# Stick-breaking attention: the two heads of a pair taken alternately, block by block, in the score and the value products

## The chip, the cores and the metric

The kernel runs on one core of a Trainium2 chip. The metric is the device time of one execution in microseconds (us), the median of several runs. PE is TensorE (matmuls), ACT is ScalarE, DVE is VectorE, POOL is GpSimd, SP is SyncE, which only issues transfers here.

## The reference, cut to what matters

The model is a stack of three blocks over 512 positions of width 1024. The first block's mixer has four retention heads and eight stick-breaking heads of width 64; the change touches only the latter.

```python
def stick_breaking(q, k, v):                      # (B, S, H, D) with S = 512, H = 8, D = 64
    ...
        z = jnp.einsum('bhid,bhsd->bhis', qi, kh).astype(jnp.float32) * scale
        past = (kpos[None, :] < qpos[:, None])[None, None]
        log_keep = jnp.where(past, jax.nn.log_sigmoid(-z), 0.0)
        between = lax.cumsum(log_keep, axis=3, reverse=True) - log_keep
        a = jnp.where(past, jnp.exp(jax.nn.log_sigmoid(z) + between), 0.0)
        return jnp.einsum('bhis,bhsd->bhid', a.astype(vh.dtype), vh)
```

## The kernel before

Everything is written by hand: each stage gives one function per engine, the functions of a block run one after another on their engine, and semaphores tie them together. No scheduler moves anything.

`stick_stage` takes the eight heads as four pairs `p`. A pair's queries `q` and keys `kk` lie on 128 partitions, head 0 of the pair on 0 to 63 and head 1 on 64 to 127; `v` has positions on the partitions, head 0 in columns 0 to 63 and head 1 in 64 to 127. On PE a pair goes through:

- scores (line 480): for each head `hh` and key block `j` (128 keys), one product of 64 partitions into 512, 384, 256 or 128 causal columns, into three PSUM banks of its own (0 to 2 for head 0, 3 to 5 for head 1). Before that PE waits for `y_out`, since the result of the pair before lies in banks 0 and 3, and head by head.
- the projections of the next pair (`project`, lines 448 and 454; parts 0, 1, 2 are q, k, v) into banks 6 and 7. Part 2 waits until ACT has moved part 0 out of its bank (`kept`).
- sums (line 493): the cumulative sums over the keys, ten products per head, after `cut`.
- values (line 503): for each head, four products of 128 partitions and 64 columns of `v` into PSUM partitions 0 to 63 of bank 0 (head 0) or 64 to 127 of bank 3 (head 1). They wait for `masked`, head by head.

Beside this ACT computes, for each head, Abs, Exp and Ln of its scores (lines 534, 536, 538), DVE adds the positive part (line 582), POOL zeroes what isn't in the past (line 558, `cut`); after the sums ACT takes the Exp (line 546) and POOL masks it (line 565, `masked`). DVE copies each head's values out of PSUM (line 574, `y_out`). ACT moves q, k (line 516) and v (line 523) out of PSUM. In fp32 the program's one matmul appears in the trace as two passes, each with its own weight load, so that the eight score products of a pair are 16 rows there.

After the last pair comes `mix_out_stage` (line 614), whose products wait for all eight `y_out`. The odd block later in the program has a product of the same kind as the scores: `score` (line 1139) issues the products of two 64-partition halves right behind each other into two banks.

Of the kernel before, what the change touches and what calls it, by code (L numbers as in the profile page):

```python
# [15 lines left out]
P = 128  # L16
S = 512
NT = S // P
# [124 lines left out]
def slab_ready(k, pe, slab, turn=0):  # L143
    slot, _, before, dmas, per = slab
    pe.wait_ge(k.landed[slot], turn * (16 * dmas * per) + 16 * (before + dmas))
# [252 lines left out]
def stick_stage(k):  # L398
# [12 lines left out]
    scored, logged, softened, cut = k.sem("sb_scored"), k.sem("sb_logged"), k.sem("sb_softened"), k.sem("sb_cut")  # L411
    summed, exped, masked = k.sem("sb_summed"), k.sem("sb_exped"), k.sem("sb_masked")
    valued, y_out = k.sem("sb_valued"), k.sem("sb_y_out")
    k.sb_y_out = y_out
    place = [(0, 0), (1, 0), (2, 0), (1, 384)]
# [9 lines left out]
    def tensor(pe):  # L425
        def project(p, part):
            n = 3 * p + part
            slabs = k.sb_slabs[p]
            if n >= 2:

                if part == 2:
                    pe.wait_ge(kept, 2 * p + 1)
                elif part == 0:
                    pe.wait_ge(kept, 2 * p)
                else:
                    pe.wait_ge(v_kept, p)
            elif part == 0:
                pe.wait_ge(k.ret_kept, 16)
                pe.wait_ge(k.ret_rotated, 16)
            bank = 6 + (n % 2)  # L440
            for c in range(KC):
                slab = slabs[c // 4]
                if part == 0 and c % 4 == 0:
                    slab_ready(k, pe, slab)
                w = k.ring[:, slab[0], 0:4 * 3 * P].rearrange("p (k n) -> p k n", k=4)[:, c % 4, :]
                w = w[:, part * P:(part + 1) * P]
                if part < 2:
                    mm = pe.matmul(PS[:, bank, :], w, k.XT[:, c, :], start=(c == 0), stop=(c == KC - 1))
            if part == 2:
                for t in range(NT):  # L450
                    for c in range(KC):
                        slab = slabs[c // 4]
                        w = k.ring[:, slab[0], 0:4 * 3 * P].rearrange("p (k n) -> p k n", k=4)[:, c % 4, :]
                        mm = pe.matmul(PS[:, bank, t * P:(t + 1) * P], k.XT[:, c, t * P:(t + 1) * P],
                                       w[:, 2 * P:3 * P], start=(c == 0), stop=(c == KC - 1))
                        if t == NT - 1 and c == 3:
                            mm.then_inc(k.freed[slabs[0][0]], 1)
            mm.then_inc(projected, 1)
            if part == 2:
                pe.drain().then_inc(k.freed[slabs[1][0]], 1)  # L460

        pe.wait_ge(k.cols_in, 1)
        pe.wait_ge(k.taps_in, 1)
        for part in range(3):
            project(0, part)
        pe.wait_ge(k.bias_masked, 1)
        for p in range(4):
            pe.wait_ge(kept, 2 * p + 2)
            for hh in range(2):
                if p > 0:  # L470
                    pe.wait_ge(y_out, 2 * (p - 1) + hh + 1)
                elif hh == 0:
                    pe.wait_ge(k.ret_masked, 16)
                    pe.wait_ge(k.ret_normed, 4)
                    pe.wait_ge(k.ret_y_out, 4)
                r = slice(64 * hh, 64 * hh + 64)
                for j in range(NT):
                    bank, col = place[j]
                    n = S - j * P
                    mm = pe.matmul(PS[:, 3 * hh + bank, col:col + n], kk[r, j * P:(j + 1) * P],  # L480
                                   q[r, j * P:S], start=(j != 3), stop=False, skip_group_check=True)
                mm.then_inc(scored, 1)
            if p < 3:
                for part in range(3):
                    project(p + 1, part)
            for hh in range(2):
                pe.wait_ge(cut, 2 * p + hh + 1)
                for j in range(NT):
                    bank, col = place[j]
                    for j2 in range(j, NT):  # L490
                        lo = (j2 - j) * P
                        n = S - j2 * P
                        mm = pe.matmul(PS[:, 3 * hh + bank, col + lo:col + lo + n],
                                       k.negtri if j2 == j else k.negone,
                                       soft[hh][:, COL[j2]:COL[j2] + n],
                                       start=False, stop=(j2 == NT - 1), skip_group_check=True)
                mm.then_inc(summed, 1)
            pe.wait_ge(v_kept, p + 1)
            for hh in range(2):
                pe.wait_ge(masked, 2 * p + hh + 1)  # L500
                r = slice(64 * hh, 64 * hh + 64)
                for j in range(NT):
                    mm = pe.matmul(PS[r, 3 * hh, j * P:S], v[:, j, r],
                                   a[hh][:, COL[j]:COL[j] + S - j * P],
                                   start=(j == 0), stop=(j == NT - 1), skip_group_check=True)
                mm.then_inc(valued, 1)

    def scalar(act):
        def keep(p):
# [59 lines left out]
    def vector(dve):  # L569
# [6 lines left out]
        for p in range(4):  # L576
# [6 lines left out]
            keep_y(p)  # L583

    return dict(sync=sync, tensor=tensor, scalar=scalar, vector=vector, gpsimd=gpsimd)

def mix_out_stage(k, name, w_out, slabs, ready, gains, mode, beside=None):
# [1987 lines left out]
```

## Time and profile before

| | |
|---|---|
| time, median of 3 runs | 2657.3 us (2656.2, 2657.3, 2662.22) |
| span of the profiled execution | 2660.7 us |
| profiled execution's own time | not listed apart; it can't be shorter than its span, so of the three only 2662.22 could be it |
| PE busy | 2367.5 us (89%) |
| DVE, ACT, POOL busy | 925.8, 685.3, 258.9 us |
| stretch of the stick-breaking scores to values | 196.42 to 341.62 us of the span |

How to read it: the page lists for each engine how long it was busy, and the timeline of one engine lists its groups of instructions in order with the idle time before each and what ended it. Neighbouring rows give the cost of a stage on PE best, as the difference of their starts: matmuls are pipelined and the tail of one lies under the next. PEclk is the clock that PE was granted, 1.00 for 2.4 GHz and 0.50 for 1.2 GHz.

### The profile page before, as it was taken

Reading aid. Unit: us, or ns where it says so; the run is one execution under the profiler, and the core shown is the slowest. Engines: PE = TensorE matmul, PEld = TensorE weight load, DVE = VectorE, ACT = ScalarE, POOL = GpSimd, SP = SyncE. Lnnn points to the kernel's source line nnn. Section 1 sums busy time; section 2 is a strip of 40 time slices with the busy share of each in tenths; the row PEclk is TensorE's granted clock in tenths of the full one; section 3 lists DMA queues with packets and bytes.
Section 4 is the critical chain, followed back from the end, with each engine's and each line's share of the span. In section 5 each row is a group of like instructions: output and inputs, shape, how many; then the busy total and the mean of one; then the engine's idle time right before and its main releaser. Section 6 shows DMA issues by size and latency. Waiting matters only on the chain. (4 is left out here: it accounts for less than half of the span.)

```text
span 2660.7 us, 25189 instructions
## 1 busy us (share of the span) xinstructions
PE 2367.5 (89%) x9090; PEld 1526.2 (57%) x9090; DVE 925.8 (35%) x1587; ACT 685.3 (26%) x930; POOL 258.9 (10%) x303
## 2 busy tenths in 40 slices
PE   8989899999979888999999784868489999999994
PEld 4456548888865555478888573654344444444442
DVE  1221135465333333355653559873300001000002
ACT  1114404344212333043432232323011111111111
POOL 1000100000000000000000035760100000000001
PEclk9999999999989999899999897879699999999997
DMA  9021108432225002043322141101099898979893
GB/s 264 24 88 39 41 16 323 136 95 97 89 72 155 32 33 64 0 119 95 96 95 95 48 111 36 48 16 35 17 386 339 307 344 290 346 290 344 300 334 139
DMA packets 286099, 385.91 MB, mean 145 GB/s; under 512 B 13512, under 2 KB 181628, under 8 KB 285880
## 3 DMA queue, kind: packets, MB, share of 16 engines
q1 hardware_dynamic: 268872, 323.54, 36.9%
q0 software_dynamic: 17136, 61.14, 6.2%
q8 instruction: 59, 0.97, 0.2%
q14 instruction: 32, 0.26, 0.0%
HBM read 347.89 MB, written 39.37 MB: 146 GB/s over the span
## 5 line engine op out<-in xcount | busy, mean ns | idle before, releaser
L845 PE MATMUL PS<-XS,split 128*128 128x512 f32 (+1 forms) x2304 | 486.1, 374 | 13.0 <-DVE split L157 9.9
L845 PEld LDWEIGHTS PS<-XS,split 128*128 128x128 f32 x2304 | 410.2, 191 | 88.6 <-issue 10.3
L2241 PE MATMUL PS<-ring,W 128*128 128x512 f32 x960 | 424.5, 598 | 6.9 <-ACT W L2287 6.9
L2241 PEld LDWEIGHTS PS<-ring,W 128*128 128x128 f32 x960 | 179.6, 191 | 223.3 <-issue 209.3
L157 DVE TENSOR_TENSOR split<-ring,split 128x2048 fp32r<-128x2048 f32 x68 | 155.7, 2292 | 219.9 <-ACT split L152 219.9
L2262 PE MATMUL PS<-ring,W 128*128 128x512 f32 x480 | 212.4, 595 | 11.3 <-ACT W L2297 11.3
L878 PE MATMUL PS<-split,XS 128*128 128x512 f32 x960 | 218.4, 389 | 0.3 <-DVE XS L157 0.3
L878 PEld LDWEIGHTS PS<-split,XS 128*128 128x128 f32 x960 | 180.0, 188 | 38.4 <-issue 1.1
L152 ACT CAST split<-ring 128x2048 fp32r<-128x2048 f32 x78 | 148.1, 1903 | 154.4 <-PE PS L878 110.8
L2314 DVE TENSOR_TENSOR W<-PS,W 128x512 f32<-128x512 f32 x30 | 20.8, 692 | 450.6 <-PE PS L2241 450.6
L614 PE MATMUL PS<-ring,W 128*128 128x512 f32 x384 | 170.3, 603 | 2.9 <-issue 0.8
L2262 PEld LDWEIGHTS PS<-ring,W 128*128 128x128 f32 x480 | 90.0, 190 | 122.4 <-issue 122.4
L1440 PE MATMUL PS<-XS,split 128*128 128x512 f32 x432 | 105.5, 405 | 24.6 <-DVE W L1753 17.3
L614 PEld LDWEIGHTS PS<-ring,W 128*128 128x128 f32 x384 | 73.5, 194 | 93.3 <-issue 90.2
L1119 PE MATMUL PS<-XT,ring 128*128 128x512 f32 x256 | 121.6, 631 | 2.0 <-PEq L2558 2.0
L263 PE MATMUL PS<-ring,XT 128*128 128x512 f32 x256 | 111.4, 593 | 1.0 <-DMA ring<-in_w_in_even 0.8
L1440 PEld LDWEIGHTS PS<-XS,split 128*128 128x128 f32 x432 | 84.2, 197 | 44.8 <-issue 20.0
L2320 DVE COPY W<-PS 128x512 f32<-128x512 f32 x60 | 38.7, 686 | 198.0 <-PE PS L2262 198.0
L1507 DVE SCALAR_TENSOR_TENSOR W<-W,chan 128x512 f32<-128x512 f32 x90 | 105.0, 1167 | 7.2 <-issue 0.4
L921 ACT ACTIVATE W<-PS,taps 128x512 f32<-128x512 f32 x88 | 67.4, 777 | 142.8 <-PE PS L845 142.7
L1119 PEld LDWEIGHTS PS<-XT,ring 128*128 128x128 f32 x256 | 51.0, 205 | 70.9 <-issue 70.5
L948 DVE SCALAR_TENSOR_TENSOR W<-PS,taps,W 128x511 f32<-128x511 f32 x88 | 65.6, 746 | 70.9 <-ACT W L921 70.9
(337 smaller groups left out, 2341.3 us busy)
## 6 DMA issues: line engine op xcount, KB each, us to landing
ring<-in_expert_w_gate SPq DMA_DIRECT2D x60, 1024.0 KB, 14.5
ring<-in_expert_w_up SPq DMA_DIRECT2D x60, 1024.0 KB, 15.4
ring<-in_expert_w_down SPq DMA_DIRECT2D x60, 1024.0 KB, 14.8
ring<-in_w_up SPq DMA_DIRECT2D x88, 512.0 KB, 5.1
ring<-in_w_down SPq DMA_DIRECT2D x44, 512.0 KB, 4.3
expert_rows<-rows POOLq DMA_DIRECT2D x4, 4096.0 KB, 30.4
expert_rows<-W POOLq DMA_DIRECT2D x30, 512.0 KB, 7.1
ring<-in_w_in_even SPq DMA_DIRECT2D x56, 256.0 KB, 5.3
```

Source lines behind the costliest of these rows:

```text
L152: act.copy(hi, raw).then_inc(sem, 1)
L157: return dve.tensor_tensor(lo, raw, hi.bitcast(F32), ALU.subtract)
L263: mm = pe.matmul(PS[:, 4 + t, :], k.XT[:, c, t * P:(t + 1) * P], w, start=(c == 0), stop=(c == KC - 1))
L614: mm = pe.matmul(k.PS[:, 2 * (t % 2) + half, :], YT[:, c, t * P:(t + 1) * P], w[:, 512 * half:512 * half + 512], start=(c == 0), stop=(c = ...
L845: mm = pe.matmul(PS[:, b + q, rows], w[:, c, q, :], x_half(k, high)[:, c, rows], start=(c == 0 and m == 0), stop=(c == KC - 1 and m == 2))
L878: mm = pe.matmul(PS[:, 2 * t + half, :], h_half(i, high)[:, at:at + P], w[:, c, 512 * half:512 * half + 512], start=(i == 0 and c == 0 and ...
L921: act.activation(conv[:, i % 2, q, :], PS[:, b + q, :], ACT.Identity, bias=tap_at(k, layer, 3, q, turn, i), scale=tap_at(k, layer, 2, q, t ...
L1119: mm = pe.matmul(PS[:, bank, :], view[c // 4][:, c % 4, part, :], k.XT[:, c, :], start=(c == 0), stop=(c == KC - 1))
L1440: mm = pe.matmul(to, part[:, c, columns], x_half(k, high)[:, c, rows], start=(c == 0 and m == 0), stop=(c == KC - 1 and m == 2))
L1507: mm = eng.scalar_tensor_tensor(acc[:, c, :], u[:, c, i - 1:i - 1 + S], wide[:, i - 1, c:c + 1], acc[:, c, :], ALU.mult, ALU.add)
L2241: mm = pe.matmul(PS[:, 2 * b + m, :], xT[b][:, 4 * half + c, :], w[:, c, :], start=(half == 0 and c == 0), stop=(half == 1 and c == 3))
L2262: mm = pe.matmul(PS[:, bank, :], midT[b][:, 2 * half + c, :], w[:, c, 512 * side:512 * side + 512], start=(half == 0 and c == 0), stop=(ha ...
```

## The change

In the scores and in the values the loop over the blocks is now outside and the loop over the two heads inside. So each head's product for a block stands right behind the other head's for the same block. The waits, which were one for each head, become one for the pair ahead of the first product: scores wait until both `y_out` of the pair before are there, values until both heads are masked. The increments (`scored`, `valued`) stay at each head's last product, which are now next to each other. ACT, DVE and POOL are unchanged.

```diff
-            for hh in range(2):
-                if p > 0:
-                    pe.wait_ge(y_out, 2 * (p - 1) + hh + 1)
-                elif hh == 0:
-                    pe.wait_ge(k.ret_masked, 16)
...
-                r = slice(64 * hh, 64 * hh + 64)
-                for j in range(NT):
-                    bank, col = place[j]
-                    n = S - j * P
+            if p > 0:
+                pe.wait_ge(y_out, 2 * p)
...
+            for j in range(NT):
+                bank, col = place[j]
+                n = S - j * P
+                for hh in range(2):
+                    r = slice(64 * hh, 64 * hh + 64)
                     mm = pe.matmul(PS[:, 3 * hh + bank, col:col + n], kk[r, j * P:(j + 1) * P],
                                    q[r, j * P:S], start=(j != 3), stop=False, skip_group_check=True)
-                mm.then_inc(scored, 1)
+                    if j == NT - 1:
+                        mm.then_inc(scored, 1)
...
             pe.wait_ge(v_kept, p + 1)
-            for hh in range(2):
-                pe.wait_ge(masked, 2 * p + hh + 1)
-                r = slice(64 * hh, 64 * hh + 64)
-                for j in range(NT):
+            pe.wait_ge(masked, 2 * p + 2)
+            for j in range(NT):
+                for hh in range(2):
+                    r = slice(64 * hh, 64 * hh + 64)
                     mm = pe.matmul(PS[r, 3 * hh, j * P:S], v[:, j, r],
                                    a[hh][:, COL[j]:COL[j] + S - j * P],
                                    start=(j == 0), stop=(j == NT - 1), skip_group_check=True)
-                mm.then_inc(valued, 1)
+                    if j == NT - 1:
+                        mm.then_inc(valued, 1)
```

On PE, from the values of pair 0 to the first projection of pair 2, the order before is (the shapes are those of the output; in brackets the semaphores waited for):

```order
135 L503 MATMUL PS<-W 64x512 [waits sb_masked,sb_v_kept]
136 L503 MATMUL PS<-W 64x384
137 L503 MATMUL PS<-W 64x256
138 L503 MATMUL PS<-W 64x128
139 L503 MATMUL PS<-W 64x512 [waits sb_masked]
...
142 L503 MATMUL PS<-W 64x128
143 L480 MATMUL PS<-W 128x512 [waits sb_y_out,sb_kept]
...
146 L480 MATMUL PS<-W 128x128
147 L480 MATMUL PS<-W 128x512 [waits sb_y_out]
...
151 L448 MATMUL PS<-XT,ring 128x512 [waits slab_landed0,sb_kept]
```

At the same place the order after is:

```order
132 L504 MATMUL PS<-W 64x512 [waits sb_masked,sb_v_kept]
133 L504 MATMUL PS<-W 64x512
134 L504 MATMUL PS<-W 64x384 x2
135 L504 MATMUL PS<-W 64x256 x2
136 L504 MATMUL PS<-W 64x128 x2
137 L480 MATMUL PS<-W 128x512 [waits sb_y_out,sb_kept]
138 L480 MATMUL PS<-W 128x512
139 L480 MATMUL PS<-W 128x384 x2
140 L480 MATMUL PS<-W 128x256 x2
141 L480 MATMUL PS<-W 128x128 x2
142 L448 MATMUL PS<-XT,ring 128x512 [waits slab_landed0,sb_kept]
```

The second wait for `sb_masked` has moved ahead of all eight value products, the second wait for `sb_y_out` ahead of all eight score products, and the heads alternate. Nothing else has moved on any engine.

## Rows read from the trace of the kernel before

**Rows 1.** The page: busy time of each engine over the span, and its share.

```profile
PE 2367.5 (89%) x9090; PEld 1526.2 (57%) x9090; DVE 925.8 (35%) x1587; ACT 685.3 (26%) x930; POOL 258.9 (10%) x303
```

**Rows 2.** Timeline of PE, the stick-breaking stage: start, us, group, [idle before, releaser].

```profile
196.42 4.00 PE L480 MATMUL PS<-W 64*128 64x512 f32 x16 [0.36 <-issue]
200.36 14.00 PE L448 MATMUL PS<-XT,ring 128*128 128x512 f32 x32
214.19 7.31 PE L454 MATMUL PS<-ring,XT 128*128 128x128 f32 x64
...
230.47 4.86 PE L503 MATMUL PS<-W 128*64 128x512 f32 x16
235.26 4.03 PE L480 MATMUL PS<-W 64*128 64x512 f32 x16
239.22 14.00 PE L448 MATMUL PS<-XT,ring 128*128 128x512 f32 x32
253.06 7.31 PE L454 MATMUL PS<-ring,XT 128*128 128x128 f32 x64
...
323.31 6.73 PE L493 MATMUL PS<-W,small 128*128 128x512 f32 x20 [6.29 <-POOL W L558]
331.40 4.60 PE L493 MATMUL PS<-W,small 128*128 128x512 f32 x20 [1.36 <-POOL W L558]
335.93 4.86 PE L503 MATMUL PS<-W 128*64 128x512 f32 x16
341.62 18.69 PE L614 MATMUL PS<-ring,W 128*128 128x512 f32 x43 [0.83 <-issue]
```

**Rows 3.** Timeline of PE's weight loads, second head's values of pair 0.

```profile
232.96 0.19 PEld L503 LDWEIGHTS PS<-W 128*64 128x64 f32 x2 [0.37 <-POOL W L565]
```

**Rows 4.** Timeline of ACT in the stage.

```profile
230.58 1.24 ACT L546 ACTIVATE W<-PS 128x1280 f32<-128x1280 f32 x1 [3.10 <-PE PS L493]
...
237.72 1.24 ACT L534 ACTIVATE W<-PS 128x1280 f32<-128x1280 f32 x1 [1.71 <-PE PS L480]
...
250.90 0.58 ACT L516 ACTIVATE W<-PS 128x512 f32<-128x512 f32 x1
```

**Rows 5.** Timeline of POOL, second head's mask of pair 0.

```profile
231.88 1.03 POOL L565 TENSOR_SCALAR_AFFINE_SELECT W<-W 128x128 f32<-128x128 f32 x4 [3.31 <-ACT W L546]
```

**Rows 6.** Timeline of DVE, the copies of the values, pair 0 and the last.

```profile
235.37 0.69 DVE L574 COPY W<-PS 64x512 f32<-64x512 f32 x1 [1.81 <-PE PS L503]
...
340.83 0.69 DVE L574 COPY W<-PS 64x512 f32<-64x512 f32 x1 [1.81 <-PE PS L503]
```

**Rows 7.** Groups by form on line 480, 236.87 to 237.40 us.

```profile
L480 PE MATMUL PS<-W x5: 269/376/693, 236.5 to 237.3; 64*128 64x256 f32 x2, 64*128 64x384 f32 x1, 64*128 64x512 f32 x1, 64*128 64x128 f32 x1
```

**Rows 8.** Timeline of PE, odd block: two heads of it.

```profile
821.60 0.92 PE L1139 MATMUL PS<-W 64*128 64x384 f32 x4
822.45 0.49 PE L1161 MATMUL PS<-W 128*128 128x128 f32 x2
825.13 0.44 PE L1151 MATMUL PS<-small,W 128*128 128x128 f32 x2 [2.20 <-DVE W L1287]
...
835.18 0.61 PE L1161 MATMUL PS<-W 128*128 128x128 f32 x4
...
858.16 0.44 PE L1151 MATMUL PS<-small,W 128*128 128x128 f32 x2 [2.21 <-DVE W L1287]
...
866.56 0.60 PE L1169 MATMUL PS<-small,W 128*128 128x128 f32 x4
```

**Rows 9.** Waits of PE, 820 to 1030 us: us in total, times, longest.

```profile
PE PS L1151 <- DVE W L1287: 15.4, 7, 2.2
```

**Rows 10.** Stretches behind those seven pauses: us, PE busy (x), PEclk, DMA share, GB/s.

```profile
826.00:829.40 3.40, 3.40 (x7) 0.50 0.43 110
858.20:861.60 3.40, 3.40 (x11) 1.00 0.01 2
...
1027.50:1030.70 3.20, 3.20 (x7) 0.50 0.00 0
```

More of the change, by code:

```diff
@@ L468, in tensor @@
             pe.wait_ge(kept, 2 * p + 2)
-            for hh in range(2):
-                if p > 0:
-                    pe.wait_ge(y_out, 2 * (p - 1) + hh + 1)
-                elif hh == 0:
-                    pe.wait_ge(k.ret_masked, 16)
-                    pe.wait_ge(k.ret_normed, 4)
-                    pe.wait_ge(k.ret_y_out, 4)
-                r = slice(64 * hh, 64 * hh + 64)
-                for j in range(NT):
-                    bank, col = place[j]
-                    n = S - j * P
+            if p > 0:
+                pe.wait_ge(y_out, 2 * p)
+            else:
+                pe.wait_ge(k.ret_masked, 16)
+                pe.wait_ge(k.ret_normed, 4)
+                pe.wait_ge(k.ret_y_out, 4)
+            for j in range(NT):
[3 more added lines that the diff above has]
+                    r = slice(64 * hh, 64 * hh + 64)
                     mm = pe.matmul(PS[:, 3 * hh + bank, col:col + n], kk[r, j * P:(j + 1) * P],
                                    q[r, j * P:S], start=(j != 3), stop=False, skip_group_check=True)
-                mm.then_inc(scored, 1)
+                    if j == NT - 1:
+                        mm.then_inc(scored, 1)
             if p < 3:
```

## The prediction

> **What bounds the kernel now.** I read the page's busy times first: PE is busy 89% of the span, no other engine over 35% [rows 1]. An average doesn't say what bounds the stage that changes, so next comes PE's own timeline there [rows 2]. From 196.42 to the scores of the last pair PE's groups follow each other with hardly a gap: scores, projections, sums, values, scores. Four pairs repeat the pattern (two handovers from values to scores lie in the part that isn't shown, the same within 0.01 us). So up to the last pair every microsecond taken from or added to PE's sequence moves the end. The last pair has no projections to lay over ACT's work: PE stands idle 6.29 us before its sums, and there the time from the scores over ACT, DVE and POOL to the sums counts. Behind it the output product at 341.62 waits for the last copy of the values. I take a shift at 341.62 as a shift of the end: from there PE goes on, and the transfers aren't what ends its waits.
>
> **Where the two heads could run side by side.** The score products use 64 of 128 partitions. At the seam between the heads the kernel before already overlaps them: in 0.53 us from 236.87 there are five passes alive on line 480, among them both 256-column passes and a 128 of head 0 and the first 512 of head 1 [rows 7]. The odd block is clearer. Its line 1139 issues two halves right behind each other, and the four passes of 384 columns, two for each half, take 0.85 us from 821.60 to the next product at 822.45 [rows 8]. One pass of 384 columns streams 384 x 2 / 2.4 GHz = 0.32 us, an estimate that fits 512-column passes of 14.00 / 32 = 0.44 us [rows 2]; so 0.85 is two passes and 0.2 of handover, not four. Two halves in full overlap, then.
>
> The Trainium skill says otherwise in one respect: in TensorE: Matmul & The Clock Gate, under Packing small matmuls, matmuls start strictly in program order. By that, head 1's first pass would have to wait for head 0's second, three passes in a row instead of two, 1.2 us for the row above. The measured 0.85 decides against it. By that rule each alternating stage below would be one 512-column pass (0.43 us) longer, which makes the sum some 3 us worse over eight stages.
>
> **The scores, four pairs.** Before, they take 200.36 - 196.42 = 3.94 and 239.22 - 235.26 = 3.96 us. One head's eight passes with the handover take 235.26 - 232.96 = 2.30 us in the values, which have the same columns [rows 2, 3]. Side by side I take 2.5, with 0.2 for the other head's weight loads between. Gain 1.45 us each. Bounds: 2.3 (gain 1.65) and 3.96 (nothing).
>
> **The values, four pairs.** Before, head 0's start at 230.47, right behind the sums, while head 1's mask isn't there: ACT's Exp starts at 230.58 and takes 1.24, POOL starts at 231.88 and takes 1.03, PE goes on at 232.96 [rows 3 to 5]. So head 0's values were what filled the wait. Now both wait: 232.96 - 230.47 = 2.49 us in which PE, with everything queued behind the wait, does nothing. Then both take 2.30 side by side, plus 0.1. The values end where they ended before: the gain is eaten by the new wait, +0.1. The bounds are 0 (full overlap) and +2.1 (none), since only partitions have been seen side by side and these products share all partitions and differ in columns; no row shows that. I take the overlap, as the nearest rows have it. The Trainium skill (TensorEngine Tiling (Array Packing), Tiling Modes) lists two column tiles as independent like row tiles; no run here shows it for fp32.
>
> **The copies.** Before, DVE copied head 0's values during head 1's products and head 1's from 235.37 to 236.06, while PE was in head 0's scores [rows 6]. Now both values end together, DVE does two copies of 0.69, the second ends at about 235.45 + 2 x 0.67 = 236.8, and the scores wait for both. They start 1.55 us later than 235.26. Queued behind on PE are the scores and all of the next projections.
>
> **One handover (pairs 0 to 1, 1 to 2).** +1.55 for the start of the scores, -1.45 for the scores: +0.1 each, +0.2 for two. A check for ACT, which gets its scores 1.55 later: it takes them at 237.72, 2.46 after the start, and leaves q by 250.90 + 0.58 = 251.48, which the v projection waits for at 253.06 [rows 2, 4]. There were 1.6 us of slack, and 0.1 remain. Cost nothing, but if I am off by 0.3 it costs the excess.
>
> **Pair 0.** Its scores wait for nothing new: -1.45, with 0.1 given back by the same wait of the v projection, which PE now reaches at 212.75: -1.35.
>
> **Pair 3.** The scores start 1.55 later, head 0's last product comes as long after the start as before (+0.05 for alternation), so ACT starts 1.6 later, and with no projections between this goes through to the sums: +1.6. The scores' gain buys idle time.
>
> **End.** Before, only one copy stood between the last value and 341.62 (340.83 + 0.69). Now two: +0.7.
>
> Sum at constant clock: -1.35 + 0.2 + 1.6 + 0.7 = +1.15 us.
>
> **The clock.** That leaves out what the pauses do. At each handover PE now stands still for about 2.4 us (from the end of the sums at 230.54), works 2.3 and stands still 1.5 more. In the odd block the trace has seven pauses of 2.2 us [rows 9]. Behind six of them the granted clock is 0.50, which is 1.2 GHz, behind one it stays 1.00, or 2.4 GHz [rows 10], where four more rows at 0.50, like the first and the last, are left out. Two heads with the same work give the price: 835.18 - 825.13 = 10.05 us with the fall, 866.56 - 858.16 = 8.40 without [rows 8], so 1.65 us. The new pauses are at least as long and there are four, in front of the values of each pair. Six in seven would be 3.4 falls; I take three, +4.95. Bounds: none (0), and four at 6.73 - 4.60 = 2.13 each, the sums of one head at low and at full clock [rows 2], +8.5.
>
> **Sum.** +1.15 + 4.95 = +6.1 us. Against the profiled execution this makes 2660.7 + 6.1 = 2666.8 of span; that execution is 3.4 us above the median, probably the one of 2662.22. Against the median: 2657.3 + 6.1 = 2663.4.
>
> **Rivals.**
> - The clock holds through the pauses (one fall at most): +1.15 to +2.8, so 2659. For it: the values between the two pauses keep PE busy, and one of seven pauses passed. Against: six of seven.
> - The values don't run side by side, column halves being unlike partition halves: 4 x 2.1 = 8.4 more, about 2671 with two or three falls. For it: no row shows such a pair at once. Against: the array overlaps the other kind fully.
> - The alternation does nothing in the scores either (each product blocks the next, whatever its half): 3.96 stays, the 1.45 is lost four times at most, less in the last pair: +4.4 more, 2668. Rows 7 and 8 speak against it.
> - Faster: the copies. If head 0's values were done well ahead of head 1's, its copy would lie under them, and if PE could start scores once the first copy is out, each pair would keep its 1.45: at four pairs -5.8, 2651.5, at constant clock. It decides from the point where the second copy ends by 235.3. With the heads alternating block by block both values end within about 0.1 us, so rows 6 speak against it. The same holds for the masks: they would have to be ready at 230.47, and Exp can't start before the sums end.
>
> **How the numbers follow.** Forecast as worked out 0.50, clock holds 0.22, values in series 0.16, nothing overlaps 0.04, faster 0.08. No change means within 0.2%, 5.3 us or 2652.0 to 2662.6, about what a measurement of this kernel can tell. The forecast's own range is 2660 to 2667 and lies astride the upper edge: 0.32 slower, 0.18 the same. The clock rival is in the same band; the two serial ones are slower. Slower 0.52, same 0.40, faster 0.08. Range for 8 in 10: 2657 to 2670.
>
> **What would show it.** In the profile after: line 480 of pair 0 some 2.5 us from its start to line 448; on line 504 an idle time of about 2.4 us ended by POOL L565 in all four pairs, then 16 passes in about 2.4 us; on line 480 an idle time of 1.4 to 1.5 ended by DVE in three; two DVE copies back to back; granted clock 0.50 in three short stretches around the values that weren't there before. It would be wrong if line 504 takes over 4 us, if the clock stays at 1.00 in the handovers, or if the output product starts before 341.6.

## The result and the profile after

The changed kernel takes 2668.33 us (median of 5 runs, 2668.12 to 2670.31) against 2657.87 us before (5 runs, 2656.2 to 2662.22): ratio 1.0037, 95% interval 1.0025 to 1.0050. That is 10.5 us more, slower by more than the 0.2% that counts here. Forecast were +6.1 us and 2663.4; the time lies inside the range of 2657 to 2670, but above the forecast's own 2660 to 2667. The five runs of before were low: three of them lie under 2658, as do 3 of the 61 that followed with the experiments, and the median over 32 and 18 of those is 2661.8 and 2661.7. The changed kernel, run again beside the 18, came at 2670.6, a ratio of 1.0030 (1.0018 to 1.0041).

The timeline of PE in the stage, after (494 is the sums and 504 the values, numbers one higher than before; those behind them, like 616, are two higher). It answers to [rows 2, 3]:

```profile
195.56 2.43 PE L480 MATMUL PS<-W 64*128 64x512 f32 x16 [0.37 <-issue]
197.91 14.00 PE L448 MATMUL PS<-XT,ring 128*128 128x512 f32 x32
211.80 7.41 PE L454 MATMUL PS<-ring,XT 128*128 128x128 f32 x64
219.32 8.93 PE L494 MATMUL PS<-W,small 128*128 128x512 f32 x40
230.77 3.89 PE L504 MATMUL PS<-W 128*64 128x512 f32 x16 [2.52 <-POOL W L567]
236.23 2.43 PE L480 MATMUL PS<-W 64*128 64x512 f32 x16 [1.57 <-DVE W L576]
238.59 14.00 PE L448 MATMUL PS<-XT,ring 128*128 128x512 f32 x32
252.47 7.41 PE L454 MATMUL PS<-ring,XT 128*128 128x128 f32 x64
259.99 8.93 PE L494 MATMUL PS<-W,small 128*128 128x512 f32 x40
271.44 4.03 PE L504 MATMUL PS<-W 128*64 128x512 f32 x16 [2.52 <-POOL W L567]
...
312.26 4.07 PE L504 MATMUL PS<-W 128*64 128x512 f32 x16 [2.52 <-POOL W L567]
317.89 2.43 PE L480 MATMUL PS<-W 64*128 64x512 f32 x16 [1.56 <-DVE W L576]
328.18 6.89 PE L494 MATMUL PS<-W,small 128*128 128x512 f32 x20 [7.87 <-POOL W L560]
336.27 4.60 PE L494 MATMUL PS<-W,small 128*128 128x512 f32 x20 [1.20 <-POOL W L560]
343.38 3.90 PE L504 MATMUL PS<-W 128*64 128x512 f32 x16 [2.51 <-POOL W L567]
348.81 11.40 PE L616 MATMUL PS<-ring,W 128*128 128x512 f32 x26 [1.53 <-issue]
```

The view of PE's waits from 190 to 350 us sums them up (us in total, times, longest):

```profile
PE PS L504 <- POOL W L567: 10.1, 4, 2.5
PE PS L494 <- POOL W L560: 9.1, 2, 7.9
PE PS L480 <- DVE W L576: 4.7, 3, 1.6
PE PS L616 <- issue: 1.5, 1, 1.5
```

Both new waits are there: in front of the values in all four pairs, ended by POOL, and in front of the scores in three, ended by DVE. The scores take 2.35 us to the next product instead of 3.94. But the values, which should take 2.4 once they start, take 3.9 to 4.1. The stretches around them show why (us, PE busy, PEclk, DMA share, GB/s):

```profile
219.40:230.30 10.90, 8.86 (x40) 1.00 0.00 0
230.50:233.80 3.30, 3.03 (x9) 0.50 0.00 0
234.10:240.00 5.90, 4.33 (x28) 1.00 0.01 3
271.50:274.70 3.20, 3.20 (x10) 0.50 0.00 0
312.50:315.70 3.20, 3.20 (x12) 0.50 0.00 0
343.20:346.40 3.20, 3.02 (x9) 0.50 0.57 211
```

The granted clock is at 1.2 GHz behind all four pauses, and at 2.4 GHz before the pause and once the scores run. It is low from the first value product on (0.50 from 230.80 to 231.50), so the second pause, in front of the scores, comes too late to be its cause. The kernel before has one such stretch in the stage, behind the last pair's pause of 6.29 us (0.50 from 323.30 to 327.60); it is there in every version below too, and no count of falls here includes it. From the first scores to the output product the stage takes 348.81 - 195.56 = 153.25 us, against 341.62 - 196.42 = 145.20: +8.05. DVE's two copies, which answer to [rows 6], now stand together:

```profile
234.68 1.41 DVE L576 COPY W<-PS 64x512 f32<-64x512 f32 x2 [21.89 <-PE PS L504]
```

### The profile page after: what moved, and what is told of

The parts are those of the page before. It is cut to its first block and busy times, and to the rows that moved or that the text cites. A ratio compares the mean times of both kernels' runs of the same rounds, so it can differ in the third digit from the quotient of the medians.

```text
span 2666.3 us, 25189 instructions
## 1 busy us (share of the span) xinstructions
PE 2357.4 (88%) x9090; PEld 1520.4 (57%) x9090; DVE 924.8 (35%) x1587; ACT 685.3 (26%) x930; POOL 259.3 (10%) x303
```

## The experiments

Stage below means the time from the start of the first scores to the start of the output product, read in each kernel's timeline of PE.

**The kernel before, a second trace.** No edit.

> The kernel before, unchanged, for a second trace. In the two traces so far the stage from the first scores to the output product grew by 153.25 - 145.20 = 8.05 us, while the medians differ by 10.4; before came at 2656 to 2658 three times and at 2662 twice. Theory A (falls of PE's clock at pauses elsewhere, which come out differently from one execution to another): a second trace has the same 145.2 us in the stage, within 0.2, and a span that differs from 2660.7 by 3 to 5 us, with the difference in stretches at clock 0.50 outside the stage. Theory B (the change costs 2 us more outside the stage, say in transfers): the second trace has again a span near 2660.7.

Median 2663.17 us (11 runs, 2658.51 to 2664.62), ratio to the other runs of before 0.9999 (0.9990 to 1.0008). Stage 341.02 - 195.81 = 145.21 us, as in the first trace. The span is 2660.0, only 0.7 from the first, so the trace itself shows no 3 to 5 us of difference; that part of theory A missed. The runs do: the same kernel ranges over 8 us. Outside the stage the two traces of before have 2515.5 and 2514.8 us, the changed kernel 2666.3 - 153.25 = 2513.1. So theory B is out, as far as one trace tells: nothing outside the stage became slower. The scatter goes with the clock: of the 61 runs of before that came with the experiments, the 8 with a mean granted clock of 0.938 take 2663.9 us on average, the 39 at 0.939 2662.3, the 12 at 0.940 2659.7 and the 2 at 0.941 2657.4. Which pauses make the difference isn't shown.

**Scores alternate, values in turn.**

```diff
-            pe.wait_ge(masked, 2 * p + 2)
-            for j in range(NT):
-                for hh in range(2):
-                    r = slice(64 * hh, 64 * hh + 64)
+            for hh in range(2):
+                pe.wait_ge(masked, 2 * p + hh + 1)
+                r = slice(64 * hh, 64 * hh + 64)
+                for j in range(NT):
```

> Only the scores alternate, behind one wait for both y_out; the values are head by head as before. Theory (pauses and clock): no pause of 2.5 us in front of the values, so no new fall of the clock. Scores take 2.35 instead of 3.95 us (-1.6). The second copy ends where it ended before, 236.06 in the old trace, so the scores start 0.85 later. Pair 0: -1.6 + 0.16 given back at the v projection. Two handovers: -0.75 + 0.15 each, so -1.2. Pair 3: +0.85. End: 0. Sum -1.8 us against before, clock 0.50 only behind the long pause of pair 3. Rival 1 (alternation itself makes the kernel slow, through the second wait for y_out): slower than before by 2 to 4. Rival 2 (the pause of 0.85 is enough for the clock): three falls more, about +3 instead of -1.8.

2660.04 us (11 runs), ratio 0.9992 (0.9983 to 1.0001), 1.75 less than before. Stage 337.07 - 193.36 = 143.71, so -1.5 for the forecast -1.8. The handover, by the timeline of PE:

```profile
225.98 4.87 PE L504 MATMUL PS<-W 128*64 128x512 f32 x16
231.73 2.43 PE L480 MATMUL PS<-W 64*128 64x512 f32 x16 [0.88 <-DVE W L575]
234.08 14.00 PE L448 MATMUL PS<-XT,ring 128*128 128x512 f32 x32
```

No pause in front of the values, one of 0.88 us in front of the scores, and the four falls are gone. This half of the change doesn't slow the kernel. In the whole time its gain is within the noise; the stage shows it.

**Values alternate, scores in turn.** The other half of the diff alone.

> Only the values alternate, behind one wait for both masks; the scores are head by head as before, each behind its own y_out. Theory (pauses and clock): the pause of 2.5 us is back in all four pairs. At constant clock the scores start 0.9 later at three handovers, since only the first copy stands between (+2.7), and the end comes 0.7 later: +3.4. Four falls at 1.75 make +7.0, sum +10.4 us against before, no less than both edits together, since the falls are all here. Rival (the falls need both pauses, the 2.5 and the 1.5 us behind it): one or two falls at most, +3.4 to +6.

2668.84 us (10 runs), ratio 1.0024 (1.0015 to 1.0034), 7.0 more than before, for a forecast of 10.4. Stage 351.14 - 197.34 = 153.80, +8.6. The four stretches around the values:

```profile
234.00:237.40 3.40, 2.57 (x17) 1.00 0.00 0
274.20:277.40 3.20, 3.20 (x12) 0.50 0.00 0
315.10:318.30 3.20, 2.96 (x8) 0.50 0.00 0
345.80:349.00 3.20, 3.20 (x12) 0.50 0.70 257
```

```profile
222.53 8.93 PE L493 MATMUL PS<-W,small 128*128 128x512 f32 x40
233.97 2.37 PE L503 MATMUL PS<-W 128*64 128x512 f32 x16 [2.51 <-POOL W L566]
237.18 4.00 PE L480 MATMUL PS<-W 64*128 64x512 f32 x16 [0.83 <-DVE W L575]
...
262.36 8.93 PE L493 MATMUL PS<-W,small 128*128 128x512 f32 x40
273.81 4.07 PE L503 MATMUL PS<-W 128*64 128x512 f32 x16 [2.51 <-POOL W L566]
278.71 4.00 PE L480 MATMUL PS<-W 64*128 64x512 f32 x16 [0.83 <-DVE W L575]
```

Three falls instead of four, behind pauses of the same 2.51 us. One pause passed, and so the kernel itself gives the price: from sums to scores 14.65 us without a fall, 16.35 with one, 1.7 us. Three of them and the 3.4 us forecast for the constant clock are 8.5 of the 8.6 us. By this trace the falls are a little cheaper, the third pair being at 320.08 - 303.90 = 16.18, and the constant part a little dearer, since the handover without a fall already takes 14.65 where it took 13.65, not 0.9 more. The forecast of 10.4 had four falls. The whole loss is in this half, and since the pause behind the values is only 0.83 here, the rival that wanted both pauses is out.

**Work laid into the pause.** In the changed kernel, ahead of the wait for the masks:

```diff
+            if p < 3:
+                pe.wait_ge(kept, 2 * p + 4)
+            spare = 6 if p == 3 else 6 + (3 * p + 4) % 2
+            for again in range(2):
+                pe.matmul(PS[:, spare, :], k.negone, k.XT[:, again, :], start=True, stop=True)
```

> The changed kernel with two products of 128x512 more per pair, which nobody reads, between the sums and the wait for the masks: four passes, about 1.75 us of work that lies in the pause of 2.5 us. Everything else is as changed. Theory (the pause costs little by itself, the clock's fall behind it costs 1.75 us each): the added work is hidden, the idle time on the values' line falls to about 0.7 us, the clock stays at 1.00 in the handovers, and the kernel is 7 us faster than the changed one though it computes more: +1 against before within the stage. Rival (the falls are not the cause, but the waits themselves): no gain against the changed kernel, +10. Second rival (only part of the falls goes, since the pause of 1.5 us behind the values remains): +3 to +6.

2663.15 us (11 runs), ratio to before 1.0005 (0.9996 to 1.0014), +1.4. Stage 340.85 - 194.03 = 146.82, +1.6, 6.4 us less than the changed kernel though it computes more.

```profile
226.56 1.88 PE L503 MATMUL PS<-XT,small 128*128 128x512 f32 x4
229.24 2.38 PE L509 MATMUL PS<-W 128*64 128x512 f32 x16 [0.80 <-POOL W L572]
233.17 2.43 PE L480 MATMUL PS<-W 64*128 64x512 f32 x16 [1.56 <-DVE W L581]
```

```profile
229.30:232.00 2.70, 2.32 (x16) 1.00 0.03 6
268.40:271.20 2.80, 2.36 (x16) 1.00 0.00 0
307.60:310.30 2.70, 2.31 (x16) 1.00 0.00 0
337.00:340.00 3.00, 2.34 (x16) 1.00 0.48 197
```

The clock stays at 1.00 in all four, and behind the pause of 1.56 us in front of the scores it doesn't fall either. This is the run that shows the cause: PE waits for the same masks and copies, and the values start 11.45 us after the sums as in the changed kernel, only PE is idle for 0.80 us of it and not 2.5. The mean clock of the runs without a trace agrees: 0.939 to 0.941 in the 11 of this version, 0.936 to 0.938 in the 12 of the changed kernel.

**The changed kernel again.** No edit.

> The changed kernel again, unchanged, beside more runs of the one before. Before has come out between 2656.9 and 2665.0 in 32 runs, so the first difference of 10.4 us may hold luck. Theory (all of the change lies in the stage): 153.2 us from the first scores to the output product again, 8.0 more than the 145.2 of both traces of before, and medians 8 us apart, within 2. Rival (2.4 us more outside the stage): medians 10 us or more apart.

2670.6 us (7 runs), 9.0 above the 2661.65 of 18 runs of before. Stage 346.15 - 192.66 = 153.49, with the same four falls. Between 8 and 10, the medians don't settle the theory against its rival. The trace speaks against the rival: 2663.2 - 153.5 = 2509.7 us outside the stage, less than in any trace of before. But it is the trace of the fastest of the seven runs, 5.4 us under their median, so it settles the stage and not the whole time.

**Useful work in both pauses.** Both products alternate; the v projection of the next pair is cut in two around the values. The last pair has the values in turn.

```diff
             if p < 3:
-                for part in range(3):
+                for part in range(2):
                     project(p + 1, part)
...
+            if p < 3:
+                project(p + 1, 2, range(3))
...
+            if p < 3:
+                project(p + 1, 2, range(3, NT))
```

> Both products alternate, but useful work is laid into both pauses: three of the four position tiles of the next pair's v projection come between the sums and the values (5.5 us), the fourth between the values and the next scores (1.85 us). In the last pair, which has no such work, the values stay head by head as before. Theory (the alternation is worth 1.6 us in the scores and 2.1 in the values of each pair where no pause replaces it): a pair takes 2.35 + 13.9 + 8.9 + 5.5 + 2.35 + 1.85 = 34.9 us instead of 38.87, so 3 x 4.0 = 12 us less than before in the stage, 133 from scores to output product, no short falls of the clock, and about 2650 where before is 2662. Rival (PE is then no longer what bounds the stage, but ACT's chain from scores to masks): less than 6 us gained, with idle time on PE ended by ACT or POOL.

2648.2 us (5 runs), ratio to before 0.9950 (0.9937 to 0.9964): faster than both kernels, by 13.5 us against before and 22 against the changed one. Stage 329.61 - 196.21 = 133.40, forecast 133.

```profile
221.08 5.52 PE L456 MATMUL PS<-ring,XT 128*128 128x128 f32 x48
226.53 2.38 PE L511 MATMUL PS<-W 128*64 128x512 f32 x16
228.83 2.05 PE L456 MATMUL PS<-ring,XT 128*128 128x128 f32 x16
231.15 2.43 PE L484 MATMUL PS<-W 64*128 64x512 f32 x16 [0.26 <-issue]
```

From 196.21 on PE has no idle row over 0.4 us until the last pair.

**The same, with the projection whole ahead of the values.**

> As the version with the v projection moved, but all four tiles of it stand between the sums and the values, so the pause of 1.5 us for the two copies, in front of the next scores, stays. Theory (a pause of 1.5 us costs its length and no fall of the clock): a pair takes 36.4 us, 7.4 us less than before in the stage, 4.5 more than with the split. Rival (the short pause lets the clock fall too): 1.7 us more at each handover, 2 us less than before.

2654.85 us (8 runs), ratio 0.9975 (0.9965 to 0.9986), -6.8. Stage 331.62 - 193.91 = 137.71, -7.5 for -7.4. The scores wait 1.56 us for DVE at three handovers, and that is what separates it from the split, 4.3 us, with no fall.

**The split, with the values in turn.** As the version before last, but with the loops over heads and blocks of the values as they were.

> As the version with the v projection laid into both pauses, but the values head by head as before. Theory (side by side is worth 2.1 us per pair in the values once nothing waits): 3 x 2.1 = 6.3 us slower than that version, 5.8 us faster than before. Rival (most of the gain comes from moving the projection, not from the alternation of the values): within 2 us of that version.

2655.26 us (9 runs), ratio 0.9974 (0.9964 to 0.9984), -6.4. Stage 332.69 - 194.52 = 138.17. The alternation of the values is worth 4.8 us here, not 6.3:

```profile
224.84 3.93 PE L510 MATMUL PS<-W 128*64 128x512 f32 x16
228.69 2.05 PE L456 MATMUL PS<-ring,XT 128*128 128x128 f32 x16
```

In turn the 16 passes take 3.85 to the next product, not 2 x 2.3, as the scores in turn take 3.94: without a wait between the heads their seam overlaps [rows 7]. So alternation saves 1.55 per pair in the values, much as in the scores. The forecast of 6.3 missed by 1.5, but the rival of less than 2 us is out.

## Why the prediction was right, and where it was off

**Overlap of the scores.** Forecast 2.5 us, measured 2.35 to the next product in three pairs, and the fourth has the same row of 2.43. The reading from the odd block [rows 8] held, and the rule of strict start order that the prediction takes from the Trainium skill (TensorE: Matmul & The Clock Gate, Packing small matmuls), which would have made it some 0.4 us longer, fails here too.

**Overlap of the values.** Taken from rows of the other kind of half, and right: 2.37 us for 16 passes at full clock, where no row of before had shown one such pair. The rival of values in series is out, by the four versions that ran them at full clock. Its price of 2.1 us per pair was too high as well: the version with the values in turn shows 1.55. In the changed kernel itself no pair shows the 2.4: the sign set in advance, that line 504 over 4 us would mean a wrong forecast, came up in two pairs (4.03 and 4.07). It was badly chosen, since it doesn't tell values in series from values side by side at the low clock, which the forecast itself expected three times.

**The wait for both masks.** Forecast 2.49, measured 230.77 - 219.32 = 11.45 against 8.86 before: 2.59. It ate the gain of the values as forecast.

**The copies.** Forecast 1.55 later for the scores. At constant clock, in the version with the filled pause, sums to scores take 233.17 - 217.79 = 15.38, 1.73 more than the 13.65 of before. This is 0.18 more than forecast, three times, and 0.10 of it is the wait for the masks.

**ACT's slack.** 0.1 us was said to remain. It was gone: ACT leaves q at 252.42, and the first weight load of the v projection waits for it:

```profile
252.47 7.22 PEld L454 LDWEIGHTS PS<-ring,XT 128*128 128x128 f32 x64 [0.71 <-ACT W L518]
```

From the projections to the sums PE takes 21.40 us where it took 21.26, in each of three pairs, 0.14 each. Small, but the step that cost nothing cost 0.4 in all (the forecast had 0.1 of it, in pair 0). It went unseen in the sum, because the scores gained 0.15 more than forecast in the same pairs: two errors that cancel, by luck.

**Pair 3 and the end.** Scores to sums 10.29 us against 10.32 before, so all of the delay went through, and the shorter scores bought idle time, 7.87 instead of 6.29. The end at constant clock is 11.00 against 10.22, +0.8 for +0.7.

**Constant clock.** Forecast +1.15. The filled version has +1.6, and none of it is the added work's as far as the rows tell: its values start 11.45 us after the sums as in the changed kernel, and its scores 3.93 after the values as in the version with the projection whole, which has no added work. So this part was 0.5 too small: 0.18 at each of three handovers, 0.1 at the end, less 0.1 in pair 0 and 0.07 between the scores and the sums of pair 3.

**The clock.** The mis-sized term: three falls at 1.65, 4.95 us. There were four in both traces of the changed kernel, and they cost 153.25 - 146.82 = 6.4 us, 1.6 each. The price was right, the number wasn't. My count was drawn down from the 3.4 that six in seven gave, without a reason in the rows. With four the sum is 1.15 + 6.6 = 7.8 for a measured 8.05. As measured, the 8.05 is 1.6 at constant clock and 6.4 of falls.

**The rest.** From 8.05 to the 10.5 of the medians there are 2.4 us that lie in no stretch of the change. The likely reason is the low first five runs of before, which isn't shown; in the later comparison the medians are 9.0 apart, with 8.3 in the stage. I named 0.2% as what can be told, and the runs of one kernel spread over more than that. So of the 4.4 us between forecast and measured change, 1.5 are the fourth fall, 0.5 the constant clock, and 2.4 stay open.

## What to carry to other kernels

Work that can run side by side wants all its inputs at once, and the wait for the last input can take back what the overlap gives: look for what the first half's work was hiding before joining the two, and put other work there. A pause of TensorE in front of short work costs its length and can cost more through the clock, here 1.6 us on top of 2.5; take the price and the frequency from pauses of that length elsewhere in the same trace. And where several shapes of the same order seem equal, the stage's own length in a trace tells 0.2 us apart where whole times scatter by 8: each of the two kernels was traced twice, and its stage came out at 145.20 and 145.21, 153.25 and 153.49 us.

## What the runs showed of the hardware that was not expected

- A pause of 2.5 us was followed by the low clock 11 times in 12 (four and four in the changed kernel's two traces, three of four with only the values alternating). The one that passed had the same length. Behind the six pauses of 1.56 us at full clock (three in the filled version, three with the projection whole) the clock never fell. A fall cost 1.5 to 1.7 us.
- Two products in column halves overlap in fp32 as fully as two in partition halves: 2.37 against 2.43 us for 16 passes of the same columns.
- The overlap begins without alternation: in turn, 16 passes take 3.93 to 4.03 us rather than twice 2.3.
- Both traces of the changed kernel have the falls behind the same four pauses. Why one of four passed with only the values alternating isn't known.
